# A decoder trunk in split fp32: the norm's gain multiplies the transposed activations instead of the weights

## The reference

```python
def rmsnorm(x, g):
    x32 = x.astype(jnp.float32)
    y = x32 * lax.rsqrt(jnp.mean(x32 * x32, axis=-1, keepdims=True) + RMS_EPS) * g.astype(jnp.float32)
    return y.astype(x.dtype)
...
    for i in range(DEPTH):
        g = norm_gains[i]
        h = rmsnorm(x, g[0])
        ...                                   # y = attention(h, w_in, ..., w_out)
        x = x + rmsnorm(y, g[1])
        h = rmsnorm(x, g[2])
        y = swiglu_ffn(h, ffn_w_gate_up[i], ffn_w_down[i])
        x = x + rmsnorm(y, g[3])
```

## Time and profile before

| | |
|---|---|
| time, median of 3 runs | 2132.51 us (2131.37 to 2133.05) |
| profiled execution: its own time | 2132.52 us |
| profiled execution: span from first to last instruction | 2130.7 us |
| TensorE busy | 2111.8 us, 99% of the span |
| VectorE busy | 1587.1 us, 74% |
| ScalarE busy | 1178.8 us, 55% |
| GpSimd busy | 122.4 us, 6% |
| DMA | 399.85 MB, 188 GB/s on average |

### The profile page before, as it was taken

How to read it: one execution, slowest core, us unless ns; L and a number is a source line. 1 busy time by engine, 2 the same in 40 slices (tenths; PEclk the granted TensorE clock), 3 DMA queues, 4 the chain that set the end, 5 groups by cost and what they waited for, 6 DMA issues and landing times.

```text
span 2130.7 us, 32456 instructions
## 1 busy us (share of the span) xinstructions
PE 2111.8 (99%) x9769; PEld 1731.5 (81%) x9769; DVE 1587.1 (74%) x3255; ACT 1178.8 (55%) x2129; POOL 122.4 (6%) x232
## 2 busy tenths in 40 slices
PE   8999999999999999999999999999999999999998
PEld 6877888888888888887878878888888888888886
DVE  6677578777668876778787787567776678776686
ACT  7677565444545444555666665665454555445452
POOL 2111000000000000000131131000000000000000
PEclk9999999999999999999999999999999999999999
DMA  8544856555665656665665565666655665556652
GB/s 257 190 128 136 217 182 210 187 187 178 200 219 187 189 175 199 197 200 160 176 199 181 180 192 169 203 204 198 195 171 185 197 216 185 188 179 198 215 192 85
DMA packets 205548, 399.85 MB, mean 188 GB/s; under 512 B 13232, under 2 KB 13392, under 8 KB 204960
## 3 DMA queue, kind: packets, MB, share of 16 engines
q1 hardware_dynamic: 203008, 390.12, 58.6%
q0 software_dynamic: 2320, 8.72, 1.4%
q10 hardware_dynamic: 144, 0.07, 0.0%
HBM read 396.72 MB, written 2.13 MB: 187 GB/s over the span
## 4 chain that ended last, share of the span: by engine, by line
PE 96%; DVE 2%; DMA 1%; issue 1%; ACT 0%; POOL 0%; SPq 0%; DVEq 0%; POOLq 0%
PE bank L1187 31%; PE bank L1189 30%; PE bank L1188 30%; PE bank L1235 1%; PE bank L1262 1%; PE bank L1246 1%; PE bank L1200 1%; DVE ring_lo L724 0%; DMA stage<-swa_w_in 0%; DMA x_sb<-x 0%; PE bank L1218 0%; DMA stage<-fox_w_in 0%; DVE x_sb L766 0%; DVE y_sb L984 0%; DVE h_t L971 0%
## 5 line engine op out<-in xcount | busy, mean ns | idle before, releaser
L1187 PE MATMUL bank<-ring_hi,a_hi 128*128 128x512 f32 x2240 | 884.5, 395 | 1.1 <-issue 0.7
L1189 PE MATMUL bank<-ring_hi,a_lo 128*128 128x512 f32 x2240 | 873.6, 390 | 0.0
L1188 PE MATMUL bank<-ring_lo,a_hi 128*128 128x512 f32 x2240 | 872.6, 390 | 0.0
L531 ACT ACTIVATE ring_hi<-stage,g_t 128x512 fp32r<-128x512 f32 x992 | 662.8, 717 | 338.5 <-DMA stage<-ffn_w_gate_up 190.6
L724 DVE SCALAR_TENSOR_TENSOR ring_lo<-stage,g_t,ring_hi 128x512 fp32r<-128x512 f32 x992 | 706.9, 758 | 166.2 <-ACT ring_hi L531 164.3
L1187 PEld LDWEIGHTS bank<-ring_hi,a_hi 128*128 128x128 f32 x2240 | 420.9, 188 | 89.7 <-issue 5.0
L1189 PEld LDWEIGHTS bank<-ring_hi,a_lo 128*128 128x128 f32 x2240 | 420.7, 188 | 89.0
L1188 PEld LDWEIGHTS bank<-ring_lo,a_hi 128*128 128x128 f32 x2240 | 421.2, 188 | 83.3
L722 DVE TENSOR_TENSOR ring_lo<-stage,ring_hi 128x512 fp32r<-128x512 f32 x480 | 306.7, 690 | 130.3 <-ACT ring_hi L529 129.1
L529 ACT ACTIVATE ring_hi<-stage 128x512 fp32r<-128x512 f32 x480 | 277.3, 623 | 167.5 <-PE bank L1189 151.1
L1187 PE MATMUL bank<-ring_hi,h_hi 128*128 128x512 f32 x704 | 274.4, 390 | 0.0
(11 more groups left out here) (132 smaller groups left out, 845.3 us busy)
## 6 DMA issues: line engine op xcount, KB each, us to landing
stage<-ffn_w_gate_up SPq DMA_DIRECT2D x352, 512.0 KB, 4.5
stage<-ffn_w_down SPq DMA_DIRECT2D x176, 512.0 KB, 5.6
stage<-fox_w_in SPq DMA_DIRECT2D x96, 512.0 KB, 4.1
stage<-swa_w_in SPq DMA_DIRECT2D x48, 512.0 KB, 4.5
stage<-swa_w_out SPq DMA_DIRECT2D x64, 256.0 KB, 4.0
stage<-fox_w_out SPq DMA_DIRECT2D x32, 512.0 KB, 4.8
g_b<-norm_gains POOLq DMA_DIRECT2D x4, 1024.0 KB, 5.6
cum_b<-cum_scratch POOLq DMA_DIRECT2D x32, 128.0 KB, 3.6
```

The lines of the kernel that those rows point to most:

```text
L531: nc.scalar.activation(ring_hi[:, n % RING, :], src, ACT.Identity, scale=g_t[:, row * KT + j:row * KT + j + 1]).then_inc(hi_ready, 1)
L1187: nc.tensor.matmul(dst, hi_a, hi_w, start=start, stop=False)
L1188: nc.tensor.matmul(dst, hi_a, lo_w, start=False, stop=False)
L1189: return nc.tensor.matmul(dst, lo_a, hi_w, start=False, stop=stop)
```

## The change

The high and low parts of all weight tiles are now made without a factor. The gain columns are applied when the transposed x is read out of PSUM. A column holds for one block of 128 x 128 only, so the one instruction for a chunk of four blocks becomes four, on ScalarE and on VectorE. ScalarE waits for `gains_made` ahead of the first chunk of x instead of behind it. The forget gate's weights are split in one instruction on each engine.

```diff
-        def gain_row(u):
-            ...
+        def norm_gain(b, k):
+
+            return g_t[:, 2 * b * KT + k:2 * b * KT + k + 1]
...
-                row = gain_row(u)
-                src = stage[:, n % STAGE, :]
-                if row is None:
-                    nc.scalar.activation(ring_hi[:, n % RING, :], src, ACT.Identity).then_inc(hi_ready, 1)
-                else:
-                    nc.scalar.activation(ring_hi[:, n % RING, :], src, ACT.Identity,
-                                         scale=g_t[:, row * KT + j:row * KT + j + 1]).then_inc(hi_ready, 1)
+                nc.scalar.activation(ring_hi[:, n % RING, :], stage[:, n % STAGE, :], ACT.Identity).then_inc(hi_ready, 1)
...
                 act.wait_ge(xt_done, n + 1)
-                nc.scalar.activation(a_hi[:, 4 * q:4 * q + 4, tok(t)],
-                                     ps[:, :].rearrange("p (k m) -> p k m", k=4), ACT.Identity).then_inc(xt_hi, 1)
+                for k in range(4):
+                    last = nc.scalar.activation(a_hi[:, 4 * q + k, tok(t)], ps[:, k * P:(k + 1) * P], ACT.Identity, scale=norm_gain(b, 4 * q + k))
+                last.then_inc(xt_hi, 1)
...
-                    for k in range(KT):
-                        nc.scalar.activation(fg_hi[:, k, :], fg_raw[:, k, :], ACT.Identity,
-                                             scale=g_t[:, 4 * KT + k:4 * KT + k + 1]).then_inc(fg_hi_made, 1)
+                    nc.scalar.activation(fg_hi, fg_raw[:, :, :], ACT.Identity).then_inc(fg_hi_made, 1)
...
+            act.wait_ge(gains_made, 1)
             x_heads(0, 0, 0)
-            act.wait_ge(gains_made, 1)
...
-                    nc.vector.scalar_tensor_tensor(out=lo, in0=src, scalar=g_t[:, row * KT + j:row * KT + j + 1], in1=hi,
-                                                   op0=ALU.mult, op1=ALU.subtract).then_inc(lo_ready, 1)
+                nc.vector.tensor_tensor(ring_lo[:, n % RING, :], stage[:, n % STAGE, :], ring_hi[:, n % RING, :].bitcast(F32),
+                                        ALU.subtract).then_inc(lo_ready, 1)
...
                 dve.wait_ge(xt_hi, n + 1)
-                hi = a_hi[:, 4 * q:4 * q + 4, tok(t)].bitcast(F32)
-                nc.vector.tensor_tensor(a_lo[:, 4 * q:4 * q + 4, tok(t)], ps[:, :].rearrange("p (k m) -> p k m", k=4),
-                                        hi, ALU.subtract).then_inc(xt_lo, 1)
+                for k in range(4):
+                    hi = a_hi[:, 4 * q + k, tok(t)].bitcast(F32)
+                    last = nc.vector.scalar_tensor_tensor(out=a_lo[:, 4 * q + k, tok(t)], in0=ps[:, k * P:(k + 1) * P],
+                                                          scalar=norm_gain(b, 4 * q + k), in1=hi, op0=ALU.mult, op1=ALU.subtract)
+                last.then_inc(xt_lo, 1)
...
-                    for k in range(KT):
-                        dve.wait_ge(fg_hi_made, k + 1)
-                        nc.vector.scalar_tensor_tensor(out=fg_lo[:, k, :], in0=fg_raw[:, k, :],
-                                                       scalar=g_t[:, 4 * KT + k:4 * KT + k + 1], in1=fg_hi[:, k, :].bitcast(F32),
-                                                       op0=ALU.mult, op1=ALU.subtract).then_inc(fg_lo_made, 1)
+                    dve.wait_ge(fg_hi_made, 1)
+                    nc.vector.tensor_tensor(fg_lo, fg_raw[:, :, :], fg_hi.bitcast(F32), ALU.subtract).then_inc(fg_lo_made, 1)
...
-                pe.wait_ge(fg_lo_made, KT)
+                pe.wait_ge(fg_lo_made, 1)
```

## The result

| | before | after |
|---|---|---|
| median, 11 executions each | 2131.46 us (2130.11 to 2133.05) | 2136.40 us (2134.15 to 2137.80) |
| ratio | | 1.0022, 95% interval [1.0014, 1.0029] |
| profiled execution: its own time, its span | 2132.52, 2130.7 us | 2136.01, 2134.2 us |

The change makes the kernel 4.9 us slower.

The account below looks back on a forecast made before the run. TensorE was taken to bound the kernel, with only three gaps of 3.4 us open to gain. From 2132.52 us, +0.15 at the start and +0.9 at the handover to U_FOX gave 2133.6 us; range 2131.0 to 2136.8 us.

Parts of the forecast that it names:

- my own mark of 4 us: Sign of failure set beforehand: the prediction is wrong if the kernel's time moves by more than 4 us.
- No change: Outcome with the time neither faster nor slower by over 0.2%, about 4.3 us; chance 0.92.
- What bounds the kernel: Whole kernel: TensorE is busy 2111.8 of 2130.7 us, so lighter work elsewhere gains only where TensorE waits.
- TensorE's three gaps: Waits of 1.47 us ending at 52.06, 0.74 at 1001.32 and 1.23 at 1008.93 us; together 3.4 us.
- The weight tiles: All 992 scaled tiles: unscaled ones save 0.09 us each on ScalarE and 0.07 on VectorE, mostly without gain in time.
- The rival that they are not lighter: Weight tiles: unscaled ones save nothing; start +0.8 us, U_FOX handover +1.8, so 2135.1 us; chance 0.10.
- A chunk on VectorE: Reading x: four narrow instructions take 1.05 us against 0.60 for one wide, so +0.45 us a chunk.
- the slower rival: Unit 0: narrow ScalarE instructions of 0.38 us or more make ScalarE the bound; 2137.6 us; chance 0.10.
- Handover to U_FOX: VectorE's order ahead of the second mean near 1009 us: residual sum, and TensorE with it, +0.9 us later.
- Both terms: VectorE's stretch ahead of U_FOX: four narrow chunks add 1.8 us, 13 lighter tiles take away 0.9 us.
- The start: First chunks up to `k_t` at 52.06 us: the wait for `gains_made` costs nothing, narrow chunks leave +0.15 us.
- The other handovers and the forget gate: Handovers at b = 1 and b = 3, and the forget gate's matmuls: enough room, so zero cost.

Follow-up runs that it names:

- e5: Changed kernel with all chunks of x wide, the gains wait back behind the first chunk and those gains left out: 2130.06 us, ratio 0.9992.
- e1: Changed kernel with one small ScalarE activation ahead of everything, so the table load runs early: 2135.43 us, ratio 1.0015.
- e10: Kernel before with three useless 512-column copies on VectorE ahead of the second mean in U_FOX: 2134.50 us, ratio 1.0007.
- e3: Changed kernel with 18 filler transposes on TensorE ahead of its wait for the residual sum in U_FOX: 2135.16 us, ratio 1.0016.
- e6: Changed kernel with the edits of e1 and e3 together: 2133.96 us, ratio 1.0010.
- e4: Kernel before with only ScalarE's wait for `gains_made` moved ahead of the first chunk of x: 2133.70 us, ratio 1.0009.
- e9: Kernel before with only the U_FOX order of e7 for the third and fourth chunks' low parts: 2131.49 us, ratio 0.9996.
- e7: e1 with U_FOX's third chunk's low part moved behind the second mean, the fourth's behind the first residual sum: 2132.43 us, ratio 1.0004.
- e2: Changed kernel with the four chunks of U_FOX's first token half read wide, without the gain: 2133.78 us, ratio 1.0007.
- e8: Kernel before with the order of e9 plus 12 early identity transposes ahead of TensorE's wait for the gains: 2130.66 us, ratio 0.9996.

## Why the prediction was right and wrong

The measured 2136.4 us lies inside the range, by its upper end, and the sign was right. The size was not: +1.1 us forecast, +4.9 measured, and by my own mark of 4 us that is wrong. That the time lies in the range is in part luck: I started from a profiled execution of 2132.52 us, 1.1 above the later median. The same range around that median would end at 2135.7 us, and 2136.4 is outside it. "No change" had 0.92 of the chance; the ratio's interval reaches from 0.14 to 0.29% and mostly lies above 0.2%, to which I had given 0.05.

- **What bounds the kernel**: right. TensorE's three gaps, 3.4 us, were all that lighter tiles could touch; e5 brought 1.5 us. TensorE's busy time rose by 1.3 us, over the 1 us that I had allowed, which is about what the low clock costs.
- **The weight tiles**: right. 0.09 and 0.06 us each: 717 to 626 ns, 758 to 693. The rival that they are not lighter fell. ScalarE's busy time fell by 67 us (70 forecast), VectorE's by 38 (50 forecast).
- **A chunk on VectorE**: 1.04 us from the first of the four to the next instruction, 1.05 forecast. On ScalarE 1.0 us, 1.2 forecast. A 128-column piece takes 376 ns on ScalarE, close to the row that the slower rival stood on, but pieces start 0.25 us apart. Distance, not duration, was the right reading. That rival fell: ScalarE waits for the transposes in all chunks together for 20.8 us. Its time, 2137.6 us, came nearer to the measured one than my forecast did, by luck, since neither of the two costs that I missed is in it. From the Trainium skill, "VectorE: DVE Perf Modes", section "The TRN2 errata", an estimate for a PSUM source of 128 columns is 0.26 us on VectorE and 0.25 on ScalarE; the trace agrees, 1.04/4 and 1.0/4. What the section says of a bubble between instructions, which I set against the change, it says of sources in SBUF, and a chunk is read from PSUM. Its table has no difference between the two forms of a tile, and there the trace, 758 against 693 ns, decides.
- **Handover to U_FOX**: the sum was right, the end of it missing. From the first tile of VectorE's stretch to the transposes it took 1008.93 - 982.95 = 25.98 us before and 1010.90 - 983.95 = 26.95 after, +0.97 against +0.9 forecast. Both terms were right: with unscaled tiles and wide chunks (e5) the stretch is 1008.17 - 982.98 = 25.19 us, so the tiles took away 0.8 (0.9 forecast), and the narrow chunks added 1.76 (1.8 forecast). The step failed at "with it TensorE after 1008.93 us, is **+0.9 us** later": I gave the longer gap no effect on what comes behind it, and it also took the clock down, another 1.5 us in the profiled execution. The two groups of e1's executions are 2.6 us apart (medians 2135.8 and 2133.2), a us more than the clock costs in a trace; that rest stays open. e10 has the fall with a longer gap and nothing narrow, and e3 and e6 show the clock kept when the gap is filled.
- **The start**: "The new wait for `gains_made` costs nothing" failed. I asked whether what it waits for is late, which it is not, and not what the wait does to the table load, that stood in the same place. Alone on the kernel before it costs 2.1 us (e4), in the changed kernel 1.0 to 1.2 (e1, e6 against e3). The first product was forecast at 9.3 us; with the load out of the way it is at 9.4 and 9.3 (e1, e6). The table below shows that the rest of the step, +0.15 us at `k_t` for the narrow chunks, is borne out as far as the scatter lets one see (52.53 against 52.27 us), and that one trace there says little: the same start scatters by 0.7 to 1.2 us.
- **The other handovers and the forget gate**: right, no gap at either, and the matmuls of the forget gate show none.

| start of the kernel | traces | first transposes behind `k_t`, us | middle one |
|---|---|---|---|
| scaled tiles, wide chunks, early table load | before, e9, e10 | 52.06, 52.27, 52.73 | 52.27 |
| unscaled tiles, narrow chunks, early table load | e7, e1, e6 | 52.02, 52.53, 52.80 | 52.53 |
| unscaled tiles, narrow chunks, late table load | after, e3, e2 | 53.20, 53.65, 54.41 | 53.65 |
| scaled tiles, wide chunks, late table load | e4 | 54.03 | |

Along one path the costs add up by the medians' distance from the kernel before: +4.9 for the change, less 1.0 for the table load (e1: +3.9), less 1.5 for the clock (e6: +2.4), less 1.5 for the order of the chunks (e7: +0.8). Each such step is smaller than the half width of one interval, 1.9 us, so their sizes are rough, and the last +0.8 is not clear of nothing. The mechanisms are shown by the traces. Whether the table load really costs more in the kernel before than in the changed one stays open: 2.1 against 1.0 to 1.2 us is within the intervals, and e4's place in the table within the scatter.

## What to carry to other kernels

Where TensorE is busy for 99%, price a change by its few gaps: 160 us of work taken off engines that were not the bottleneck brought 1.5 us, while small additions ahead of those gaps cost three times that. Ask of a gap not only how much longer it gets but what it does to the clock behind it; a few dummy matmuls in the gap, or two instructions moved behind the mean, are cheap cures. A wait added ahead of ScalarE's first activation held back the table load here; one small activation ahead of it kept the load early.

## What was not expected of the hardware

The same gap does not always take the clock down. Gaps of 1.0 to 1.25 us (before, e2, e4, e5) left it at 1.00, and so did 2.34 us in e1; gaps of 2.36 us (after) and 2.23 us (e10) took it to 0.50 for over 3 us. Nor does it fall in the gap itself each time. The means of the windows put the fall at 1010.8 us in the changed kernel, just ahead of the transposes, and at 1010.6 in e10, 0.7 us after TensorE had work again; both figures are estimates from 0.91 and 0.78 in the window from 1010 to 1011 us. The changed kernel's executions lie 3.7 us apart; e3's, with the gap filled, 1.8. At the start products run 0.43 us apart while the granted clock is given as 1.00 (this window of the changed kernel), so there the distance of the products tells more than that column. In e8, where the rate had been high before, the column does show the fall, 0.52 from 8 to 9 us.

```profile
10.00:12.00 2.00, 1.61 (x4) 1.33 (x5) 2.00 (x4) 1.74 (x5) 0.00 (x0) 1.00 1.06 408
```
